# Expert products of a two-layer backbone: plain FP32 on 32-column tiles in place of three products of split halves on the full array

## Chip, cores and metric

The kernel runs on one core of a Trainium2 chip. The metric is the device time of one execution in microseconds (us); lower is better. Five engines matter here: PE (TensorE, matrix products), DVE (VectorE), ACT (ScalarE), POOL (GpSimd) and SP (SyncE, which here only issues transfers). Matrix products are written to PSUM (eight banks `ps[0]` to `ps[7]`, each 128 partitions by 512 FP32 columns); everything else lies in SBUF.

## What is computed

The reference runs 256 latent tokens and 256 context tokens, 1024 wide, through two layers of mixers (attention, pooling, Fourier) and a feed-forward part. In layer 0 the feed-forward part is dense; in layer 1 it is this mixture of experts over the 256 latent tokens, which the change touches:

```python
def swiglu(h, w1, w3, w2):
    return (jax.nn.silu(h @ w1) * (h @ w3)) @ w2

def moe_swiglu(h, w_router, b_router, w1, w3, w2):
    logits = (h @ w_router).astype(jnp.float32) + b_router.astype(jnp.float32)
    top_v, top_i = lax.top_k(logits, TOP_K)            # TOP_K = 2
    top_w = jax.nn.softmax(top_v, axis=-1)
    combine = jnp.sum(jax.nn.one_hot(top_i, N_EXPERTS) * top_w[..., None], axis=-2)
    out = jnp.zeros_like(h)
    for e in range(N_EXPERTS):                          # 8 experts, 1024 -> 2816 -> 1024
        out = out + combine[..., e:e + 1] * swiglu(h, w1[e], w3[e], w2[e])
    return out
```

All is FP32. With the reference's own inputs its router gives the eight experts 74, 80, 50, 73, 56, 53, 60 and 66 of the 256 tokens (each token goes to two).

## The kernel before

Everything up to the router is untouched by the change, but for the places of buffers. The expert stage comes last but for the final norm. It works on the tokens of one expert after the other: a table `sel` of ones and zeros picks them, products with it gather them into at most `SLOTS` = 128 rows, and, when an expert's rows are done, products with the turned table `selT` scatter them back (`gather`, `turned_select`, `scatter`). If any expert had more than `SLOTS` tokens, a second pass over all experts would run (`If(most_r[0] > SLOTS)`).

The weights of the experts come from memory in units of 1 MB (128 partitions by 2048 FP32), 33 units an expert, 264 in all, each read once. SP issues them in a fixed order into 11 landing buffers `estage` (L688); a buffer is free when DVE has read it (`e_lo_done`).

Precision is got by splitting: PE multiplies the type FP32R in one pass with fewer bits, so every FP32 operand is held as a high half (rounded to FP32R) and a low half (the rest), and three products stand for one: high x high, high x low, low x high. For the weights this is done anew for each unit: ACT writes the high half `ehi` (L992), then DVE writes the low half `elo` as the difference (L1548); both have three buffers (`SPLIT`). For the gathered tokens the halves are `xg_hi` and `xg_lo`, for the hidden rows `ehT_hi` and `ehT_lo`.

An expert is cut into 11 chunks of 256 hidden columns. A chunk has three units: "ga" and "gb" (the `w1` and `w3` columns of the chunk, four blocks of 128 rows each; `up`, L2204 to L2206: 12 products of 512 columns a unit) and "w" (256 rows of `w2`; `down`, L2218, L2219, L2224: 12 products of 512 columns). Between them ACT takes the silu (L1056), DVE multiplies by the other half of the bank (L1606), PE turns the 128 x 256 result with two transposes (`turn`, L2188), ACT and DVE split it (L1022, L1571). `down` of a chunk runs one chunk later than its `up`, so that PE need not wait for that.

At a few points of each expert PE does the other work: `gather` in two parts (8 products of 512 columns, L2160; 8 transposes, L2166), `turned_select` (L2179, L2181) and `scatter` (16 products of 256 columns, L2242, L2243), with the rows scaled and split by ACT (L1034) and DVE (L1580) beforehand.

After the last expert PE runs a few filling products (`keep_clock`, L1807), the last rows are scaled and split (L1091, L1648), scattered (L2306, L2307), added (L1657), squared (L734), summed (L1787) and normed.

One more place of the kernel is needed for the argument: `early_rows` (L1760 to L1770), near the start. It multiplies plain FP32 operands with only 32 columns on the weight side, and gives each of four such products its own quarter of the output partitions of one bank:

```python
for i in range(KD // quarters):                    # 2
    for q in range(quarters):                      # 4
        ins = pe.matmul(ps[2 + g][TILE_W * q:TILE_W * (q + 1), :], cond_32[:, k, :], w, ...)   # TILE_W = 32
```

Of the kernel before, what the change touches and what calls it, by code (L numbers as in the profile page):

```python
# [28 lines left out]
ACT = mybir.ActivationFunctionType  # L29
# [38 lines left out]
STAGE = 11  # L68
SPLIT = 3
# [37 lines left out]
assert UNITS % STAGE == 0 and UNITS % SPLIT == 0 and EXPERTS % PAIR == 0  # L107


SCATTER_AT = (1, 2)  # L110
GATHER_AT = (4, 6)
# [107 lines left out]
def direct_stream():  # L219
# [28 lines left out]
    "e_in": 16 * MOE_UNITS // STAGE, "e_hi_done": MOE_UNITS, "e_lo_done": MOE_UNITS, "e_used": MOE_UNITS,  # L248
    "et": _CHUNKS, "eu": _CHUNKS, "tr_full": _CHUNKS, "ehT_hi": _CHUNKS, "ehT_lo": _CHUNKS,
    "sel": 2 * EXPERTS, "ga_full": 2 * EXPERTS, "xrow": 2 * (EXPERTS - 1), "gt_full": 2 * EXPERTS, "xg_hi": 2 * EXPERTS, "xg_lo": 2 * EXPERTS,  # L250
    "st_full": EXPERTS, "selT": EXPERTS, "w_slot": EXPERTS,
    "y_hi_e": 2 * (EXPERTS - 1), "y_lo_e": 2 * (EXPERTS - 1), "sc_full": 4 * (EXPERTS - 1), "x_add": KD * (EXPERTS - 1),
}


def expert_steps(x):

    for c in range(CHUNKS):
        cc = x * CHUNKS + c
        for n, kind in enumerate(STEPS):  # L260
            if cc == 0 and kind == "w":
                continue
            yield (3 * cc - 1 + n if cc else n), cc, c, kind
# [41 lines left out]
def build(nc, A):  # L305
# [53 lines left out]
    warm = fixed.take("warm", [P, 2])  # L359
# [105 lines left out]
    ehi = ex.take("ehi", [P, SPLIT, 4 * 512], F32R)  # L465
    elo = ex.take("elo", [P, SPLIT, 4 * 512], F32R)

    et = ex.take("et", [P, 2, CW])
    eu = ex.take("eu", [P, 2, CW])
    ehT_hi = ex.take("ehT_hi", [P, 2, 2, SLOTS], F32R)  # L470
    ehT_lo = ex.take("ehT_lo", [P, 2, 2, SLOTS], F32R)
# [11 lines left out]
    posm = htok.take("posm", [P, 2, 2, 2 * EXPERTS])  # L483
# [4 lines left out]
    xg_hi = htok.take("xg_hi", [P, 2, KD, SLOTS], F32R)  # L488
    xg_lo = htok.take("xg_lo", [P, 2, KD, SLOTS], F32R)
# [84 lines left out]
    def pool_bank(g):  # L574

        return ps[(4, 5, 2, 3)[g]]

# [40 lines left out]
    def _(sp):  # L618
# [64 lines left out]
        def experts(p):  # L683

            def load(v0, w, at):

                sp.wait_ge(S("e_lo_done"), passed("e_lo_done", p) + v0 + (w + 1))
                sp.dma_start(estage[:, w % STAGE, :], at).then_inc(S(f"e_in{w % STAGE}"), 16)  # L688

            with sp.Fori(0, EXPERTS // PAIR) as e2:  # L690
                v0 = e2 * (PAIR * UNITS)
                for w in range(PAIR * UNITS):
                    load(v0, w, A["moe"][bass.ds(v0 + w, 1)].rearrange("a p n -> p (a n)"))
# [4 lines left out]
        with sp.If(most_r > SLOTS):  # L698
            experts(1)
# [7 lines left out]
    def _(act):  # L707
# [275 lines left out]

        act.sem_inc(S("e_used"), SPLIT)

        def experts(p):
            used = S("e_used")

            def hi(v0, w):
                act.wait_ge(S(f"e_in{w % STAGE}"), passed("e_in", p) + v0 * 16 + 16 * (w // STAGE + 1))  # L990
                act.wait_ge(used, passed("e_used", p) + v0 * STAGE + (w + 1))
                act.activation(ehi[:, w % SPLIT, :], estage[:, w % STAGE, :], ACT.Copy).then_inc(S("e_hi_done"), 1)  # L992

            def gathered_rows(e, x):

                for f in range(2):
                    act.wait_ge(S("ga_full"), passed("ga_full", p) + e * 2 + (2 * x + f + 1))
                    act.activation(xrow[:, f * 512:f * 512 + 512], ps[5 + f][:, :], ACT.Copy).then_inc(S("xrow"), 1)

            def first_hi(f):  # L1000

                act.wait_ge(S("ga_full"), passed("ga_full", p) + f + 1)
                act.activation(xg_hi[:, 0, 4 * f:4 * f + 4, :], ps[3 + f][:, :].rearrange("p (k s) -> p k s", s=SLOTS), ACT.Copy)\
                    .then_inc(S("xg_hi"), 1)

            def gathered_hi(e, x):

                for f in range(2):
                    act.wait_ge(S("gt_full"), passed("gt_full", p) + e * 2 + (2 * x + f + 1))
                    act.activation(xg_hi[:, x % 2, 4 * f:4 * f + 4, :], ps[5 + f][:, :].rearrange("p (k s) -> p k s", s=SLOTS), ACT.Copy)\  # L1010
                        .then_inc(S("xg_hi"), 1)

            def turned_select(e, x):

                act.wait_ge(S("st_full"), passed("st_full", p) + e + (x + 1))
                act.activation(selT[:, x % 2, :], ps[7][:, 0:SEQ], ACT.Copy).then_inc(S("selT"), 1)
                act.activation(w_slot[:, x % 2:x % 2 + 1], ps[7][:, SEQ:SEQ + 1], ACT.Copy).then_inc(S("w_slot"), 1)

            def hidden_hi(c_, pc):

                act.wait_ge(S("tr_full"), passed("tr_full", p) + c_ + (pc + 1))
                act.activation(ehT_hi[:, pc % 2, :, :], ps[2][:, pc % 2 * 256:pc % 2 * 256 + 256].rearrange("p (b s) -> p b s", s=SLOTS), ACT.Copy)\  # L1022
                    .then_inc(S("ehT_hi"), 1)

            def rows_hi(e, x, v0, w):

                act.wait_ge(used, passed("e_used", p) + v0 * STAGE + (SPLIT + w + 1))
# [1464 lines left out]
```

## Time and profile before

| | |
|---|---|
| time, median of 3 runs | 1940.72 us (1939.68 to 1941.45) |
| time of the profiled execution | 1937.46 us |
| its span | 1935.7 us |
| PE busy | 98% of the span |
| DVE busy | 71% |
| ACT busy | 51% |
| bytes moved by DMA | 438.21 MB |
| granted TensorE clock, mean | 0.997 |

The span runs from the first to the last instruction; the time has 1.76 us more around it. A row of the trace gives the start in us, the duration in us, the engine (PE for products, PEld for the weight loads that go ahead of each, SPq for SP's queue), the line of the kernel, what is written and read (buffer numbers left out) and how many rows were merged (x8). In brackets stands how long the engine was idle before it and what released it. One plain FP32 product of the program shows as two rows, each with its weight load; a product of FP32R operands shows as one. Ends of products are modelled, so the distance between starts tells more than their durations.

### The profile page before, as it was taken

The page shows a single profiled execution, that of the slowest core. Times are in us where ns is not written, and L with a number is a line of the kernel's source. Part 1 is how long each engine was busy: PE and PEld are TensorE (multiplying, and loading weights), DVE is VectorE, ACT ScalarE, POOL GpSimd, SP SyncE. Part 2 cuts the span into 40 slices and gives each one's busy share as a digit, 9 for nine tenths or more (in the row PEclk, how much of TensorE's full clock was granted, in tenths as well). Part 3 has the DMA queues.
Part 4 walks back from the last instruction along what each step waited for, and adds up shares of the span by engine and source line. Part 5 has one row for each costly group of instructions (what it writes and reads, how often), then busy time and mean ns, then how long its engine had stood idle before and what let it go on. Part 6 is the DMA issues. An engine that isn't in the chain of part 4 may idle for free.

```text
span 1935.7 us, 23955 instructions
## 1 busy us (share of the span) xinstructions
PE 1902.3 (98%) x9306; PEld 1525.0 (79%) x9306; DVE 1368.2 (71%) x1624; ACT 985.4 (51%) x1087; POOL 99.9 (5%) x127
## 2 busy tenths in 40 slices
PE   8999999999999999999999999999999999999997
PEld 6776666668788888878788988888888888888886
DVE  3783444477767555556454578989898989898996
ACT  4433323322432123243443377777777777777775
POOL 0160000000000001004000000000000000000000
PEclk9999999999999999999999999999999999999999
DMA  9412222354456557414334299989898999999990
GB/s 380 149 69 77 77 76 78 134 169 152 141 164 200 170 183 251 161 55 142 130 110 164 81 406 345 366 344 368 338 373 335 371 343 363 349 355 352 358 353 24
DMA packets 72834, 438.21 MB, mean 226 GB/s; under 512 B 9232, under 2 KB 10000, under 8 KB 28560
## 3 DMA queue, kind: packets, MB, share of 16 engines
q1 hardware_dynamic: 61056, 393.65, 54.1%
q0 software_dynamic: 11664, 43.00, 6.8%
q8 instruction: 76, 1.25, 0.3%
q14 instruction: 38, 0.31, 0.0%
HBM read 435.57 MB, written 1.05 MB: 226 GB/s over the span
## 4 chain that ended last, share of the span: by engine, by line
PE 91%; DVE 4%; ACT 3%; issue 1%; DMA 1%; SPq 0%; ACTq 0%; DVEq 0%
PE ps L1746 12%; PE ps L1747 12%; PE ps L1748 12%; PE ps L2204 8%; PE ps L2206 8%; PE ps L2205 8%; PE ps L2017 6%; PE ps L2218 4%; PE ps L2219 4%; PE ps L2224 4%; PE ps L1966 2%; PE ps L1923 2%; DVE wlo L1114 1%; PE ps L1992 1%; PE ps L1977 1%
## 5 line engine op out<-in xcount | busy, mean ns | idle before, releaser
L1548 DVE TENSOR_TENSOR elo<-estage,ehi 128x2048 fp32r<-128x2048 f32 x264 | 604.6, 2291 | 74.8 <-ACT ehi L992 74.0
L992 ACT ACTIVATE ehi<-estage 128x2048 fp32r<-128x2048 f32 x264 | 505.7, 1916 | 119.0 <-PE ps L2206 70.7
L1746 PE MATMUL ps<-h_hi,whi 128*128 128x512 f32 (+1 forms) x960 | 369.4, 385 | 10.2 <-DVE h_lo L1154 4.3
L1748 PE MATMUL ps<-h_hi,wlo 128*128 128x512 f32 (+1 forms) x960 | 344.9, 359 | 0.0
L1747 PE MATMUL ps<-h_lo,whi 128*128 128x512 f32 (+1 forms) x960 | 344.8, 359 | 0.0
L2204 PE MATMUL ps<-ehi,xg_hi 128*128 128x512 f32 x704 | 282.7, 402 | 1.0 <-DVE elo L1548 1.0
L2206 PE MATMUL ps<-ehi,xg_lo 128*128 128x512 f32 x704 | 275.4, 391 | 0.0
L2205 PE MATMUL ps<-elo,xg_hi 128*128 128x512 f32 x704 | 275.0, 391 | 0.0
L1114 DVE TENSOR_TENSOR wlo<-stage,whi 128x2048 fp32r<-128x2048 f32 x79 | 184.0, 2329 | 86.1 <-ACT whi L717 86.1
L717 ACT ACTIVATE whi<-stage 128x2048 fp32r<-128x2048 f32 x79 | 150.8, 1909 | 163.8 <-PE ps L1748 163.7
L1746 PEld LDWEIGHTS ps<-h_hi,whi 128*128 128x128 f32 x960 | 181.5, 189 | 54.1 <-issue 15.1
L1747 PEld LDWEIGHTS ps<-h_lo,whi 128*128 128x128 f32 x960 | 181.7, 189 | 35.8 <-issue 10.5
L1748 PEld LDWEIGHTS ps<-h_hi,wlo 128*128 128x128 f32 x960 | 181.5, 189 | 27.4
L2206 PEld LDWEIGHTS ps<-ehi,xg_lo 128*128 128x128 f32 x704 | 132.2, 188 | 28.1
L2204 PEld LDWEIGHTS ps<-ehi,xg_hi 128*128 128x128 f32 x704 | 132.3, 188 | 25.7 <-DVE elo L1548 1.4
L2205 PEld LDWEIGHTS ps<-elo,xg_hi 128*128 128x128 f32 x704 | 132.6, 188 | 24.3
L2218 PE MATMUL ps<-ehi,ehT_hi 128*128 128x512 f32 x352 | 137.9, 392 | 1.4 <-DVE elo L1548 0.9
L2219 PE MATMUL ps<-elo,ehT_hi 128*128 128x512 f32 x352 | 137.0, 389 | 0.0
L2017 PE MATMUL ps<-br,dw 128*128 128x512 f32 (+1 forms) x384 | 131.6, 485 | 0.0
L1241 DVE SCALAR_TENSOR_TENSOR gw<-gw,crow 128x1024 f32<-128x1024 f32 x80 | 98.8, 1244 | 25.3 <-DMA gw<-in_mods 25.3
L2224 PE MATMUL ps<-ehi,ehT_lo 128*128 128x512 f32 x352 | 108.4, 389 | 0.0
L2017 PEld LDWEIGHTS ps<-br,dw 128*128 128x128 f32 x384 | 71.0, 189 | 40.2 <-issue 34.5
(248 smaller groups left out, 2328.3 us busy)
## 6 DMA issues: line engine op xcount, KB each, us to landing
estage<-in_moe SPq DMA_DIRECT2D x264, 1024.0 KB, 5.1
stage<-in_split SPq DMA_DIRECT2D x79, 1024.0 KB, 5.2
gw<-in_mods POOLq DMA_DIRECT2D x80, 512.0 KB, 4.0
dw<-in_direct SPq DMA_DIRECT2D x36, 512.0 KB, 3.8
mw_a<-in_early SPq DMA_DIRECT2D x8, 512.0 KB, 7.9
mw_b<-in_early SPq DMA_DIRECT2D x8, 512.0 KB, 15.4
xT<-in_x SPq DMA_DIRECT2D x4, 512.0 KB, 5.4
gw<-in_cond_rows SPq DMA_DIRECT2D x1, 1024.0 KB, 17.7
```

The source lines that it names most:

```text
L992: act.activation(ehi[:, w % SPLIT, :], estage[:, w % STAGE, :], ACT.Copy).then_inc(S("e_hi_done"), 1)
L1114: dve.tensor_tensor(wlo[:, u % DENSE_SPLIT, :, :], stage[:, u % DENSE_STAGE, :].rearrange("p (b c) -> p b c", c=P), whi[:, u % DENSE_SPLIT ...
L1548: dve.tensor_tensor(elo[:, w % SPLIT, :], estage[:, w % STAGE, :], ehi[:, w % SPLIT, :], ALU.subtract)\
L1746: pe.matmul(out, hi, rhs_hi, start=first, stop=False)
L1747: pe.matmul(out, hi, rhs_lo, start=False, stop=False)
L1748: ins = pe.matmul(out, lo, rhs_hi, start=False, stop=last)
L2017: ins = pe.matmul(ps[1][:, 0:T - lc], dw[:, slot, 4 * (m % 2) + k, :], br[:, b, k, lc:T], start=(k == 0), stop=(k == KB - 1))
L2204: pe.matmul(o, xg_hi[:, x % 2, kk, :], hi[:, cols], start=(kk == 0), stop=False)
L2205: pe.matmul(o, xg_hi[:, x % 2, kk, :], lo[:, cols], start=False, stop=False)
L2206: ins = pe.matmul(o, xg_lo[:, x % 2, kk, :], hi[:, cols], start=False, stop=(kk == KD - 1))
L2218: pe.matmul(ps[3 + f][:, :], a_hi, hi[:, cols], start=first, stop=False)
L2219: pe.matmul(ps[3 + f][:, :], a_hi, lo[:, cols], start=False, stop=False)
```

## The change

The halves of the expert operands go: `up` and `down` multiply plain FP32 operands straight from the landing buffers, so `ehi`, `elo`, `xg_hi`/`xg_lo` and `ehT_hi`/`ehT_lo` and the work that made them are gone. `SLOTS` is 96, in three tiles of 32 tokens. A product takes 32 tokens on the weight side and has a quarter of the output partitions; four of them, with four different column blocks of the unit, fill the 128 partitions of a bank. An expert has three chunks (of 1024, 896 and 896 hidden columns): products of `up` have 512 columns in the first chunk and 448 in the others, those of `down` have 512. There are 35 units an expert and 280 in all, 16 of the 35 having 1792 columns instead of 2048, so the bytes stay the same. Each unit still has 12 products. The tokens' sums of `up` now stand with the hidden columns spread over the four quarters, so that DVE can turn them with one transpose of 32 x 32 blocks for each chunk (`gated`) and PE's `turn` is gone. The output rows of `down` come out in parts in two banks; `part_rows` on DVE puts them together (three copies, two additions) before they are scaled. A landing buffer is free when PE has read it (`e_used`); there are 14, of which the last three may be filled first when `htok_lo` is done. The gathered tokens are copied once instead of split. The final scatter uses four banks, and all sums of squares come behind it.

```diff
-STAGE = 11
-SPLIT = 3
+STAGE = 14
+LATE = 3
+TOK = 32
...
-CW = 256
-CHUNKS = FF // CW
-STEPS = ("ga", "gb", "w")
-UNITS = len(STEPS) * CHUNKS
-SLOTS = 128
+SLOTS = 96
+PASSES = -(-SEQ // SLOTS)
+TILES_E = SLOTS // TOK
+QUADS = P // TOK
+HWS = (256, 224, 224)
+CHUNKS = len(HWS)
+BLOCKS = [hw // TOK for hw in HWS]
+STARTS = [QUADS * sum(HWS[:c]) for c in range(CHUNKS)]
...
+DOWNS = [[(0, b) for b in range(8)], [(1, b) for b in range(6)], [(1, 6)] + [(2, b) for b in range(7)]]
+UNITS = CHUNKS * KD + sum(BLOCKS) // 2
...
-                sp.wait_ge(S("e_lo_done"), passed("e_lo_done", p) + v0 + (w + 1))
+                    sp.wait_ge(S("e_used"), passed("e_used", p) + v0 + (w + 1))
+                    if w == STAGE - LATE:
+                        sp.wait_ge(S("htok_lo"), 4)
...
-                act.activation(ehi[:, w % SPLIT, :], estage[:, w % STAGE, :], ACT.Copy).then_inc(S("e_hi_done"), 1)
...
+            def silu(c_, v0, x, c, upto):
+
+                cc = x * CHUNKS + c
+                act.wait_ge(used, passed("e_used", p) + v0 * STAGE + (STAGE + upto))
+                for t in range(TILES_E):
+                    act.activation(et[:, cc % 2, t * HWS[c]:(t + 1) * HWS[c]], up_bank(x, c, t)[:, 0:HWS[c]], ACT.Silu).then_inc(S("et"), 1)
...
-                dve.tensor_tensor(elo[:, w % SPLIT, :], estage[:, w % STAGE, :], ehi[:, w % SPLIT, :], ALU.subtract)\
...
+        def part_rows(done, count):
+
+            for n, (b, q) in enumerate(((3, 3), (4, 0), (4, 3))):
+                dve.tensor_copy(y_d[n * TOK:(n + 1) * TOK, :], ps[b][q * TOK:(q + 1) * TOK, :]).then_inc(done, 1)
+            for n in (1, 2):
+                rows = slice(n * TOK, (n + 1) * TOK)
+                dve.wait_ge(done, count + n + 1)
+                dve.tensor_tensor(y_d[rows, :], y_d[rows, :], ps[4][rows, :], ALU.add).then_inc(done, 1)
+            dve.wait_ge(done, count + 5)
...
+            def gated(c_, x, c):
+
+                cc, n = x * CHUNKS + c, HWS[c]
+                for t in range(TILES_E):
+                    dve.wait_ge(S("et"), passed("et", p) + c_ * TILES_E + (TILES_E * cc + t + 1))
+                    cols = slice(t * n, (t + 1) * n)
+                    dve.tensor_tensor(eu[:, cc % 2, cols], et[:, cc % 2, cols], up_bank(x, c, t)[:, n:2 * n], ALU.mult).then_inc(S("eu"), 1)
+                dve.wait_ge(S("eu"), passed("eu", p) + c_ * TILES_E + TILES_E * (cc + 1))
+                dve.transpose(ehT[:, c, 0:TILES_E * n], eu[:, cc % 2, 0:TILES_E * n]).then_inc(S("ehT"), 1)
...
-                    pe.matmul(o, xg_hi[:, x % 2, kk, :], hi[:, cols], start=(kk == 0), stop=False)
-                    pe.matmul(o, xg_hi[:, x % 2, kk, :], lo[:, cols], start=False, stop=False)
-                    ins = pe.matmul(o, xg_lo[:, x % 2, kk, :], hi[:, cols], start=False, stop=(kk == KD - 1))
+            def landed(v0, w):
+
+                pe.wait_ge(S(f"e_in{w % STAGE}"), passed("e_in", p) + v0 * 16 + 16 * (w // STAGE + 1))
+                return estage[:, w % STAGE, :]
+
+            def up(v0, w, x, c, kk):
+
+                rows, n = landed(v0, w), 2 * HWS[c]
+                for t in range(TILES_E):
+                    for q in range(QUADS):
+                        ins = pe.matmul(up_bank(x, c, t)[q * TOK:(q + 1) * TOK, 0:n], xg[:, x % 2, kk, t * TOK:(t + 1) * TOK],
+                                        rows[:, q * n:(q + 1) * n], start=(kk == 0), stop=(kk == KD - 1))
...
+            def down(v0, w, d):
+
+                for u in range(len(DOWNS[d]) // 2):
+                    rows = landed(v0, w + u)
+                    two = DOWNS[d][2 * u:2 * u + 2]
+                    first, last = (d, u) == (0, 0), d == CHUNKS - 1 and u == len(DOWNS[d]) // 2 - 1
+                    for i, (c, b) in enumerate(two):
+                        for q in range(QUADS):
+                            t, f = (q, 0) if q < TILES_E else (0, 1)
+                            pe.matmul(ps[3][q * TOK:(q + 1) * TOK, :], turned(c, b, t), rows[:, i * D + f * 512:i * D + f * 512 + 512],
+                                      start=(first and i == 0), stop=(last and i == 1))
+                    for q in range(QUADS):
+                        t, i = 1 + q // 2, q % 2
+                        ins = pe.matmul(ps[4][q * TOK:(q + 1) * TOK, :], turned(*two[i], t), rows[:, i * D + 512:i * D + D], start=first, stop=last)
+                    ins.then_inc(used, 1)
```

## Rows read from the trace of the kernel before

**Rows 1.** The page: busy tenths of PE and DMA in 40 slices.

```profile
PE   8999999999999999999999999999999999999997
...
DMA  9412222354456557414334299989898999999990
```

**Rows 2.** Stretches: from:to, length, engines' busy us (instructions), clock, DMA share, GB/s.

```profile
1133.30:1917.30 784.00, 780.94 (x3618) 643.94 (x3616) 702.25 (x549) 582.14 (x504) 0.00 (x0) 1.00 0.89 342
...
1450.00:1550.00 100.00, 100.00 (x467) 82.71 (x466) 90.50 (x71) 74.41 (x65) 0.00 (x0) 1.00 0.92 354
```

**Rows 3.** The page's costliest groups: busy us, mean ns, idle before, releaser.

```profile
L1548 DVE TENSOR_TENSOR elo<-estage,ehi 128x2048 fp32r<-128x2048 f32 x264 | 604.6, 2291 | 74.8 <-ACT ehi L992 74.0
...
L2204 PE MATMUL ps<-ehi,xg_hi 128*128 128x512 f32 x704 | 282.7, 402 | 1.0 <-DVE elo L1548 1.0
```

**Rows 4.** Order of time: two neighbouring expert products of 512 columns.

```profile
1502.44 0.39 PE L2204 MATMUL ps<-ehi,xg_hi 128*128 128x512 f32 x1
...
1502.67 0.39 PE L2205 MATMUL ps<-elo,xg_hi 128*128 128x512 f32 x1
```

**Rows 5.** Order of time, near the start: packed FP32 products of L1769.

```profile
15.21 0.16 PEld L1769 LDWEIGHTS ps<-mw_a,cond 128*32 128x32 f32 x8 [2.22 <-DMA mw_a<-in_early]
...
15.67 0.13 PEld L1769 LDWEIGHTS ps<-mw_a,cond 128*32 128x32 f32 x4 [0.30 <-issue]
16.10 0.13 PEld L1769 LDWEIGHTS ps<-mw_a,cond 128*32 128x32 f32 x4 [0.30 <-issue]
17.07 0.52 PEld L1787 LDWEIGHTS ps<-ones,sq_ends 128*128 128x128 f32 x4 [0.84 <-issue]
...
35.78 0.40 PE L1748 MATMUL ps<-h_hi,wlo 128*128 128x512 f32 x1
...
36.11 1.92 PE L1769 MATMUL ps<-mw_b,cond 128*32 128x512 f32 x16
...
37.97 0.50 PE L1746 MATMUL ps<-h_hi,whi 128*128 128x512 f32 x1
```

**Rows 6.** Stretches, columns as in the second group: DMA engines full.

```profile
15.00:24.00 9.00, 8.62 (x66) 4.79 (x67) 1.31 (x7) 1.01 (x3) 0.00 (x0) 1.00 1.03 418
...
1115.00:1150.00 35.00, 34.06 (x231) 30.27 (x230) 26.16 (x47) 26.95 (x35) 0.00 (x0) 1.00 1.01 425
```

**Rows 7.** Order of time, layer 1: 256-column products, then 64 weight columns.

```profile
1014.84 0.28 PE L1746 MATMUL ps<-h_hi,whi 128*128 128x256 f32 x1
...
1014.96 0.28 PE L1747 MATMUL ps<-h_lo,whi 128*128 128x256 f32 x1
...
1017.74 0.42 PEld L1992 LDWEIGHTS ps<-pT,v_a 128*64 128x64 f32 x8 [0.33 <-issue]
...
1018.12 0.47 PEld L1992 LDWEIGHTS ps<-pT,v_b 128*64 128x64 f32 x8
...
1018.76 0.42 PEld L1977 LDWEIGHTS ps<-ident,prob 128*128 128x128 f32 x4 [0.17 <-issue]
```

**Rows 8.** Order of time: first expert weights issued, first expert product.

```profile
1109.64 64.80 SPq L688 DMA_DIRECT2D estage<-in_moe  x25
...
1133.34 0.19 PEld L2204 LDWEIGHTS ps<-ehi,xg_hi 128*128 128x128 f32 x1
```

**Rows 9.** Order of time: an expert's eight transposes.

```profile
1195.49 1.03 PE L2166 MATMUL ps<-ident,xrow 128*128 128x128 f32 x8
```

**Rows 10.** Groups by line, expert stage: what follows an `up` product.

```profile
L1606 DVE TENSOR_TENSOR eu<-et,ps 128x256 f32<-128x256 f32 x88 | 36.4, 413 | 0.9 <-ACT et L1056 0.9
...
L1056 ACT ACTIVATE et<-ps 128x256 f32<-128x256 f32 x88 | 33.8, 384 | 63.6 <-PE ps L2206 63.6
```

**Rows 11.** Order of time, after the last expert product.

```profile
1917.29 1.27 ACT L1091 ACTIVATE y_rows<-ps,w_slot 128x512 fp32r<-128x512 f32 x2 [3.15 <-PE ps L2224]
1918.01 1.41 DVE L1648 SCALAR_TENSOR_TENSOR y_rows<-ps,w_slot,y_rows 128x512 fp32r<-128x512 f32 x2 [3.41 <-ACT y_rows L1091]
...
1920.02 0.36 PE L2306 MATMUL ps<-selT,y_rows 128*128 128x256 f32 x1
```

More of the change, by code:

```diff
@@ L698, in _ @@
         with sp.If(most_r > SLOTS):
-            experts(1)
+            for p in range(1, PASSES):
+                experts(p)
         for name, count, k in (("out_d", 2, 2), ("out_a", 2, 0), ("out_d", 4, 6), ("out_a", 4, 4)):
@@ L1096, in _ @@
         with act.If(most_r[0] > SLOTS):
-            last_rows_hi("fx")
-            experts(1)
-        last_rows_hi("fn")
+            for p in range(1, PASSES):
+                last_rows_hi(p, "fx", p - 1)
+                experts(p)
+        last_rows_hi(1, "fn", 0)
         for k in range(KD):
@@ L1526, in most_of_all @@
         def most_of_all():
-            step(dve.tensor_scalar(posm[:, 1, :, 0:EXPERTS], place, float(SLOTS), None, ALU.subtract))
+            for n in range(1, PASSES):
+                step(dve.tensor_scalar(posm[:, n, :, 0:EXPERTS], place, float(n * SLOTS), None, ALU.subtract))
             dve.wait_ge(S("most_full"), 1)
@@ L1663, in _ @@
         with dve.If(most_r[0] > SLOTS):
[L1664 to L1668 removed]
+            for p in range(1, PASSES):
+                last_rows_lo(p, "fx", p - 1)
+                last_adds("fx", p - 1)
+                experts(p)
+        last_rows_lo(1, "fn", 0)
+        last_adds("fn", 0)
         norm("fin", SEQ)
@@ new lines, in first_gather, with gather_rows @@
+                    ins.then_inc(S("gt_full"), 1)
+            def gather_rows(e, x):
+                pe.wait_ge(S("sel"), passed("sel", p) + e * 2 + 2 * (x + 1))
+                if x >= 2:
+                    pe.wait_ge(S("x_add"), passed("x_add", p) + e * KD + (KD * (x - 2) + 6))
+                else:
+                    pe.wait_ge(S("eu"), passed("eu", p) + TILES_E)
+                for f in range(2):
+                    for t in range(2):
+                        for n, rows in enumerate((htok_hi, htok_lo)):
+                            ins = pe.matmul(ps[6 + f][0:SLOTS, :], sel[:, t, :], rows[:, t, f * 512:f * 512 + 512],
+                                            start=(t == 0 and n == 0), stop=(t == 1 and n == 1))
+                    ins.then_inc(S("ga_full"), 1)
@@ L2266, in expert @@
+                            pe.wait_ge(S("xg"), passed("xg", p) + e * 2 + 2 * (x + 1))
+                        if (x, c) not in ((0, 0), (0, 1)):
+                            pe.wait_ge(S("eu"), passed("eu", p) + c_ * TILES_E + TILES_E * (x * CHUNKS + c))
+                        for kk in range(KD):
+                            if c == 1 and kk == KD // 2 and x >= 1:
+                                scatter(e, x, (0, 1, 2))
+                            up(v0, w + kk, x, c, kk)
                         if c == 1:
@@ L2322, in _ @@
         with pe.If(most_r[0] > SLOTS):
-            last_scatter("fx")
-            experts(1)
+            for p in range(1, PASSES):
+                last_scatter("fx", p - 1)
+                experts(p)
         keep_clock(2, 6)
-        last_scatter("fn")
-        for k in range(KD // 2, KD):
+        last_scatter("fn", 0)
+        for k in range(KD):
             last_squares(k)
```

458 lines of the change are left out of this document (191 added, 267 removed).

## The prediction, made before the change was run

> **What bounds the kernel now.** I read the page's slices first: PE is busy in all of them, and DMA is at 9 tenths only in the last two fifths, the expert stage [rows 1]. Then the stretches [rows 2]: from the first expert product to the last, 784 us, PE is busy for 781, DVE for 702, ACT for 582, at full granted clock, and the DMA engines move 354 GB/s in mid-stage at a share of 0.92. Three resources are near their ends, so the question is which wait ends last. The groups answer [rows 3]: PE waits 1.0 us in all for DVE's low halves ahead of L2204, while DVE waits 74 us for ACT, and ACT in turn for PE. So PE sets the pace, DVE (2.29 us a unit) has some slack, and the loads follow as buffers come free. The 90% of DVE that the change frees is not the bound and by itself is worth nothing. What PE does is: 264 units x 12 products = 3168 products, one every 0.23 us. Their starts are 0.23 apart to two digits [rows 4]; over a run of ten the trace gives 0.2275. That is 720.7 us of the 784. The rest: 176 turns at 0.11 (eight transposes in 1.03 us less the tail of the last, about 0.87 [rows 9]) are 19.4; per expert change, of which there are seven, the gather's 8 products (1.82), 8 transposes (0.87), the turned selection (0.7) and 16 scatter products of 256 columns at 0.12 [rows 7] (1.92) are 5.3, so 37; the last 7 us are small waits and the first expert's selection.
>
> **What the new products cost.** The packed form is in the trace of before already: `early_rows` multiplies plain FP32 with 32 weight columns, four products to a bank, 512 columns each [rows 5]. Eight products (16 rows of the trace) begin at 15.21; their weight loads come as eight, then four at 15.67 and four at 16.10. A round of four tiles thus takes 0.43 us for one of the two halves of a product (0.46 for the first one, which starts the run), 0.86 for four whole products. So four tiles truly run side by side. DMA was full at that time, 418 GB/s [rows 6], which is the company that the expert products will have. A unit has 12 products, three rounds: 2.58 us at 512 columns; 2.26 at 448 (scaled by columns; an estimate). Per expert 8 + 11 units of 2.58 and 16 of 2.26 are 85.1 us, for eight experts 681. Against 720.7 + 19.4 for products and turns now, that is 59 less. This is smaller than it looks: 96 slots in place of 128 and four passes in place of three cancel, and the gain is the 14 ns by which an FP32R product exceeds its share of the columns, and the turns.
>
> **What is added on PE.** Packed and full products alternate. From the packed ones to a full one: 36.11 to 37.97 is 1.86 for eight products that should take 1.72, so 0.14; into them: 35.78 to 36.11 is 0.33 where 0.23 was due, so 0.10 [rows 5]. Each expert change has three excursions (scatter, the last scatter with the gather, the turned rows): 7 x 3 x 0.24 = 5. Gather, turned rows, selection and scatter keep their counts: 37. For small waits I keep 4 of the 7. Stage: 681 + 37 + 5 + 4 = 727, which is 57 less than 784. Its start stays at 1133.3 [rows 8]: the first gather, not the halves of the weights, is the long part before it.
>
> **What lies beside.** ACT: three silus a chunk at about 0.38, DVE three multiplications at 0.41 [rows 10], and a turning of 768 columns, for which no row exists: between 0.86 us (elementwise by the 2.29 us for 2048 columns [rows 3]) and three times that. Together 3 to 5 us, covered by the `down` that stands between two `up`s, 3 or 4 units or 7.7 to 10.3 us. The next `up` waits only for the multiplications. If that cover failed, each of 24 chunks would cost what is over it. The joined output rows (`part_rows`, five steps of 512 columns, each at most 0.75 as a DVE step of 128 x 512 [rows 11]), then scaling and splitting, take some 5.5 us; four units of `up` (9 us) cover them before the scatter, and DVE has nothing else queued there but the next selection. The three additional landing buffers, and SP's wait for `htok_lo` with all later loads behind it, cost nothing as long as the first 11 units feed PE: they are issued from 1109.64, and PE starts 24 us later [rows 8].
>
> **The loads.** 276.8 MB remain. PE at full pace takes 1.05 MB in 2.58 us or 0.92 in 2.26, 406 GB/s, and 381 over the stage. With buffers asked for as fast as they come, the engines moved 425 GB/s for 35 us, with all of ACT's and DVE's splitting beside them [rows 6]. So they can follow, with a margin of 5% at the peak and 11% in the mean, and 14 buffers to smooth it.
>
> **After the last product.** Before: last product's end 1917.3, second low half 1919.4 [rows 11]. After: five steps of DVE (3.5 us), two scalings of 0.75 with ACT's second between: 5.0. So 3 us more. Scatter into four banks, then all squares at the end: what one saves the other costs, I take zero. A clock falling in that gap would be one more us or two, so 3 to 5.
>
> **The sum.** 57 - 3 = 54 less. The profiled execution has 1937.46; 1883.5. The median shown is 3.3 above it: 1887.
>
> **Rivals.**
>
> *Partial gain, because the loads or the rounds are slower.* The DMA rate in mid-stage is 354 at a share of 0.92 [rows 2], 385 at a full share, not 425. At 385 the mean demand of 381 is barely met, and little changes; at 360 the 276.8 MB from 1109.6 take 769 us, end at 1878.6, and PE ends some 3 us later, 21 us later than forecast: 1908. For it: a share of 0.92 looks nearly full. Against: the 425 of rows 6. Or each half round takes the 0.46 of the first instead of 0.43: 681 becomes 729, time 1935, no change. Against: the second and third are at 0.43, and the end at 17.07 fits 0.43.
>
> *Slower, because the sequencer of PE can't feed it.* A unit now has 12 weight loads and 12 products; then 24 and 24, in 2.58 us, one each 54 ns; in the 448-column units one each 47 ns. The quickest long run of the trace is a pair each 0.12 us, 60 ns a row [rows 7], and though weight loading explains that too, no long run shows less. At 60 ns a unit takes 2.88 us, 280 of them 806; with 46 us of the rest 852, which is 68 more than now, with 3 behind it 71: 2012. It decides above 55 ns a row (280 x 48 x 0.055 + 46 = 785). Against it: 16 loads and 16 products with 64 weight columns go by from 1017.74 to 1018.76, 32 ns each [rows 7]. That is a short burst, which a queue could have held ready, as it could the 32 of `early_rows`.
>
> The Trainium skill (TensorE: Matmul & The Clock Gate, on the back-to-back floor) gives a sequencer cost of about 62 ns per matmul where decoding is not done in hardware. If it counts for products alone, an estimate by it is 24 x 62 ns = 1.5 us a unit, and nothing changes; if for weight loads too, it is 3.0 us a unit and the kernel is slower by this rival's mechanism.
>
> *Slower, because four tiles aren't four times as fast in a long run.* Were a round 1.08 us instead of 0.86, the products would take 681 x 1.26 = 855 us, the stage 901, the time 2061. It decides above 0.93 us a round (46 us over 681 is 7%, and turns the gain to nothing with the tail's 3). Against: rows 5, where two rounds fit 0.86 each; but two rounds are all that there is.
>
> The same page (Measured speedup vs the span model) speaks against the change: three 32-column tiles gave 2.38 times, not 3. Read as a steady rate, 79% of the ideal, it is this rival, at 1.08 us a round. The trace doesn't bear it out at its two rounds.
>
> *The change doesn't do what it says.* Above 96 tokens in one expert a second pass would read all weights again, some 700 us. The router's largest count for the reference's inputs is 80, so I give it no chance.
>
> **How the numbers follow.** Forecast, 1868 to 1900: 64%. Partial gain, 1900 to 1935: 16%, of which a fifth lies within 0.2% of 1940.7. Sequencer, about 2010: 12%. Tiles, about 2060: 5%. Better than 1868 (no cost of the excursions, no waits): 3%. The range has to keep 8 in 10: 1866 to 1928 holds the forecast and most of the partial gain; the two slower rivals are left out. About 0.2% is what a measurement here can tell from no change. Faster 0.80, same 0.03, slower 0.17.
>
> **What would show it.** Weight loads of the new `up` in fours 0.43 us apart (0.38 in the second and third chunk), and a stretch of the stage with PE's weight loading far less busy. The stage 727 us long. ACT and DVE below a third. DMA at 380 GB/s in mid-stage. PE's waits: hardly any for `eu`, `ehT` or `estage`. If PE's idle time ahead of `up` names DMA, the loads are the bound; if it names nothing ("issue") and the fours stand further apart than 0.43, it is the sequencer or the tiles: at 448 columns the sequencer would make them as far apart as at 512, slow tiles would not. Wrong I would be, above all, if two rounds of packed products don't tell what a thousand do.

## The result and the profile after

The changed kernel takes 1887.3 us (median of 4 runs, 1882.9 to 1889.9) against 1940.5 before (the runs of "Time and profile before" and one more): a ratio of 0.9726, with a 95% interval from 0.9714 to 0.9738. The profiled execution has 1886.42 us, its span 1884.6.

The page of the changed kernel, cut to its line of busy times and the lines that answer to [rows 1] and [rows 3]:

```profile
PE 1852.9 (98%) x12682; PEld 1135.7 (60%) x12682; DVE 773.4 (41%) x1305; ACT 452.7 (24%) x719; POOL 99.9 (5%) x127
...
PE   8999999999999999999999999999999999999997
PEld 5776666667788888887788994333333333333334
DVE  3683444478667645545655451020202020202022
...
DMA  9422212255255546532333449999999999999980
...
L2204 PE MATMUL ps<-estage,xg 128*32 128x448 f32 (+1 forms) x4608 | 459.1, 557 | 0.0
...
L2204 PEld LDWEIGHTS ps<-estage,xg 128*32 128x32 f32 x4608 | 148.9, 110 | 302.4 <-issue 301.3
L1599 DVE TENSOR_TENSOR eu<-et,ps 128x224 f32<-128x224 f32 (+1 forms) x72 | 24.4, 394 | 502.8 <-ACT et L1050 502.8
```

PE is as busy as before, and its idle time ahead of the packed products (L2204) is nothing. DVE falls from 71 to 41% of the span and is nearly idle in the expert stage; PE's weight loading falls from 8 tenths to 3. Two stretches of the stage, with the columns of [rows 2]: DMA now moves 377 to 384 GB/s in mid-stage where it moved 354.

```profile
1450.00:1550.00 100.00, 100.00 (x958) 35.27 (x958) 16.89 (x35) 8.37 (x22) 0.00 (x0) 1.00 0.97 377
1550.00:1650.00 100.00, 100.00 (x978) 34.46 (x970) 14.27 (x29) 6.33 (x17) 0.00 (x0) 1.00 0.98 384
```

The rhythm itself: weight loads of the upward products in order of time, four at a time, as in [rows 5].

```profile
1400.04 0.13 PEld L2204 LDWEIGHTS ps<-estage,xg 128*32 128x32 f32 x4 [0.30 <-issue]
1400.46 0.13 PEld L2204 LDWEIGHTS ps<-estage,xg 128*32 128x32 f32 x4 [0.30 <-issue]
1400.89 0.13 PEld L2204 LDWEIGHTS ps<-estage,xg 128*32 128x32 f32 x4 [0.30 <-issue]
```

Loads of four, 0.43 us apart, after hundreds of such rounds: what two rounds of `early_rows` showed holds in a long run. And one expert change with its three stops, in order of time (PE only):

```profile
1430.08 9.20 PE L2204 MATMUL ps<-estage,xg 128*32 128x448 f32 x96
1439.21 0.38 PE L2242 MATMUL ps<-selT,y_rows 96*128 96x256 f32 x1
...
1440.83 9.23 PE L2204 MATMUL ps<-estage,xg 128*32 128x448 f32 x96
1449.98 0.39 PE L2242 MATMUL ps<-selT,y_rows 96*128 96x256 f32 x1
...
1452.53 1.92 PE L2222 MATMUL ps<-estage,ehT 128*32 128x512 f32 x16
...
1462.85 18.22 PE L2204 MATMUL ps<-estage,xg 128*32 128x448 f32 x192
1481.01 0.88 PE L2179 MATMUL ps<-ident,xrow 96*128 96x96 f32 x8
...
1482.29 1.92 PE L2222 MATMUL ps<-estage,ehT 128*32 128x512 f32 x16
...
1490.04 20.78 PE L2204 MATMUL ps<-estage,xg 128*32 128x512 f32 x192
1510.64 1.90 PE L2222 MATMUL ps<-estage,ehT 128*32 128x512 f32 x16
```

Eight units of 448 columns take 18.16 us (1462.85 to 1481.01), 2.27 each with the way out of them; eight of 512, which run on into packed products of `down`, take 20.60 (1490.04 to 1510.64), 2.575 each. The three stops (PE leaving the packed products for work on the full array) cost what lies between the end of one packed run and the start of the next: 1.67 us (a run of four units from 1430.08 would end at 1439.16; the next starts at 1440.83), 2.62 and 1.28, together 5.57.

The first expert product and what follows the last one, to set beside [rows 8] and [rows 11]:

```profile
1137.89 18.66 PE L2204 MATMUL ps<-estage,xg 128*32 128x512 f32 x172
...
1859.65 1.04 PE L2226 MATMUL ps<-estage,ehT 128*32 128x512 f32 x8
1860.76 0.68 ACT L1094 ACTIVATE y_rows<-ps,w_slot 96x512 fp32r<-96x512 f32 x1 [15.65 <-PE ps L2226]
1860.76 2.13 DVE L1554 COPY y_d<-ps 32x512 f32<-32x512 f32 x3 [15.74 <-PE ps L2226]
1861.54 1.60 PE L1814 MATMUL ps<-ident,ones 128*128 128x128 f32 x12 [0.85 <-issue]
1862.92 1.40 DVE L1558 TENSOR_TENSOR y_d<-y_d,ps 32x512 f32<-32x512 f32 x2
...
1865.91 0.47 PE L2304 MATMUL ps<-selT,y_rows 96*128 96x256 f32 x1 [2.76 <-DVE y_rows L1654]
1866.18 0.42 PE L2305 MATMUL ps<-selT,y_rows 96*128 96x256 f32 x1
...
1869.38 6.82 PE L1794 MATMUL ps<-ones,sq_fin 128*128 128x1 f32 x32
```

The stage runs from 1137.9 to 1860.5 (1859.65 and two half rounds of 0.43; a half round is one row from each of the four tiles, since a product shows as two rows), 722.6 us, and the tail to the end of the span takes 24.1. Before it was 784.0 and 18.4, counted to the first reading of the last sums (1917.3); counted to the end of the last product, as here, 783.8 and 18.6.

### The profile page after: what moved, and what is told of

It reads as the page before. It is cut to its first block, busy times and chain, and to the rows that moved or that the text cites. A ratio compares the mean times of both kernels' runs of the same rounds, so it can differ in the third digit from the quotient of the medians.

```text
span 1884.6 us, 29697 instructions
## 1 busy us (share of the span) xinstructions
PE 1852.9 (98%) x12682; PEld 1135.7 (60%) x12682; DVE 773.4 (41%) x1305; ACT 452.7 (24%) x719; POOL 99.9 (5%) x127
## 4 chain that ended last, share of the span: by engine, by line
PE 92%; DVE 4%; ACT 2%; issue 1%; DMA 1%; SPq 0%; ACTq 0%; DVEq 0%
PE ps L2204 24%; PE ps L1753 12%; PE ps L1755 12%; PE ps L1754 12%; PE ps L2222 8%; PE ps L2024 7%; PE ps L2226 4%; PE ps L1973 2%; PE ps L1930 2%; DVE wlo L1120 1%; PE ps L1999 1%; PE ps L1984 1%; ACT whi L743 1%; PE ps L1952 1%; PE ps L1938 1%
## 5 line engine op out<-in xcount | busy, mean ns | idle before, releaser
L2204 PE MATMUL ps<-estage,xg 128*32 128x448 f32 (+1 forms) x4608 | 459.1, 557 | 0.0
L2204 PEld LDWEIGHTS ps<-estage,xg 128*32 128x32 f32 x4608 | 148.9, 110 | 302.4 <-issue 301.3
L1599 DVE TENSOR_TENSOR eu<-et,ps 128x224 f32<-128x224 f32 (+1 forms) x72 | 24.4, 394 | 502.8 <-ACT et L1050 502.8
L2222 PE MATMUL ps<-estage,ehT 128*32 128x512 f32 x1408 | 167.5, 593 | 0.0
L1050 ACT ACTIVATE et<-ps 128x224 f32<-128x224 f32 (+1 forms) x72 | 21.2, 367 | 561.1 <-PE ps L2204 561.1
L2222 PEld LDWEIGHTS ps<-estage,ehT 128*32 128x32 f32 x1408 | 44.2, 110 | 99.2 <-issue 98.6
L2226 PE MATMUL ps<-estage,ehT 128*32 128x512 f32 x704 | 91.6, 592 | 0.0
L1753 PE MATMUL ps<-u_hi,whi 128*128 128x512 f32 x176 | 68.5, 389 | 0.0
L1754 PE MATMUL ps<-u_lo,whi 128*128 128x512 f32 x176 | 68.5, 389 | 0.0
L1755 PE MATMUL ps<-u_hi,wlo 128*128 128x512 f32 x176 | 68.5, 389 | 0.0
L1688 POOL DMA_DIRECT2D gw<-in_mods x80 | 42.4, 530 | 421.6 <-DVE gw L1247 407.7
```

Of the source, the lines that this page charges most:

```text
L1688: pool.dma_start(gw[:, u % 2, :], A["mods"][u]).then_inc(S(f"mod_in{u % 2}"), 16)
L1753: pe.matmul(out, hi, rhs_hi, start=first, stop=False)
L1754: pe.matmul(out, hi, rhs_lo, start=False, stop=False)
L1755: ins = pe.matmul(out, lo, rhs_hi, start=False, stop=last)
L2204: ins = pe.matmul(up_bank(x, c, t)[q * TOK:(q + 1) * TOK, 0:n], xg[:, x % 2, kk, t * TOK:(t + 1) * TOK], rows[:, q * n:(q + 1) * n], start ...
L2222: pe.matmul(ps[3][q * TOK:(q + 1) * TOK, :], turned(c, b, t), rows[:, i * D + f * 512:i * D + f * 512 + 512], start=(first and i == 0), st ...
```

## Experiments

The theory: PE sets the pace on both sides; the packed plain FP32 products run at the rate of their columns, and the gain is that rate against 0.2275 us for each FP32R product, and the turns. Its rivals: the loads, the sequencer of PE, tiles that don't truly overlap, and, for the size of the gain, DVE's work. Kernels whose name begins with a_ change the changed kernel, those with b_ the one before. The two-tile kernel, the one with the other order and the three with cut columns were run once each; the executions of one kernel spread over up to 10 us here (1881.6 to 1891.1 for the changed one), so of those five only differences well above that count.

**Do the tiles overlap: two tiles instead of four.**

```diff
-ins = pe.matmul(up_bank(x, c, t)[q * TOK:(q + 1) * TOK, 0:n], ...
+ins = pe.matmul(up_bank(x, c, t)[q % 2 * TOK:(q % 2 + 1) * TOK, 0:n], ...
```

> The changed kernel with the upward products on two column tiles instead of four (the second two column blocks are added onto the first two, so the hidden part is another; as many products, columns and bytes as before). If four tiles really run side by side, two take twice as long: half a round's four products 0.86 us instead of 0.43, the stage 454 us longer, 2341. If the gain came from something else than the tiles, the time changes by less than that; if from nothing in them, 1887.

2338.0 us, against 2341 expected. Weight loads of this kernel in order of time:

```profile
1399.96 0.12 PEld L2204 LDWEIGHTS ps<-estage,xg 128*32 128x32 f32 x2 [0.26 <-issue]
1400.34 0.12 PEld L2204 LDWEIGHTS ps<-estage,xg 128*32 128x32 f32 x2 [0.26 <-issue]
1400.71 0.12 PEld L2204 LDWEIGHTS ps<-estage,xg 128*32 128x32 f32 x2 [0.26 <-issue]
```

Two loads each 0.375 us (448 columns) where four tiles have four in 0.38. So the speed of the upward products goes with the number of tiles at work: with two of them the kernel is 20% slower than the one before.

**Does it depend on the order of the products.**

```diff
-                for t in range(TILES_E):
-                    for q in range(QUADS):
+                for q in range(QUADS):
+                    for t in range(TILES_E):
```

> The changed kernel with the two loops of the upward products swapped: for one column tile after the other its three products come together, instead of one product for each of the four tiles by turns. Same products, same sums. If each tile has a queue of its own, or PE looks far enough ahead, tiles still overlap: 1887. If products start in the order of the program and a tile takes one at a time, six halves of 0.43 us follow each other on a tile before the next tile gets work, and neighbours overlap only by one: some 9 us a unit instead of 2.58, and a time of 2800 to 3100. In between lies a limited look ahead.

2091.0 us, 204 more than the changed kernel, between the two expectations. Neither of the two limiting cases holds. Weight loads in order of time, then PE with a run of four units:

```profile
1400.05 0.17 PEld L2204 LDWEIGHTS ps<-estage,xg 128*32 128x32 f32 x4 [0.24 <-issue]
1400.46 0.14 PEld L2204 LDWEIGHTS ps<-estage,xg 128*32 128x32 f32 x2 [0.24 <-issue]
1400.83 0.17 PEld L2204 LDWEIGHTS ps<-estage,xg 128*32 128x32 f32 x4 [0.24 <-issue]
...
1410.34 14.17 PE L2204 MATMUL ps<-estage,xg 128*32 128x448 f32 x96
1424.44 0.39 PE L2242 MATMUL ps<-selT,y_rows 96*128 96x256 f32 x1
```

Six loads each 0.78 us, where eight would go by: about three tiles at work instead of four, so 3.12 us a unit. On all upward products (455 us in the changed kernel) that is a third more, 152 us. The rest lies at the ends of each run of products, where fewer tiles have work: four units take 14.10 us and not 12.5, 1.6 more, and with four such runs an expert that is some 51. Together 203. So products of other tiles do start while one tile has more of its own to do, but not without limit; how PE does that, no run here shows. Taking turns among the tiles, as the change does, is a part of what makes it pay; it is worth 204 us here.

**Is PE's sequencer near: fewer columns for each product.** Half of them here; in the second kernel a quarter (`// 4` in both places).

```diff
-                rows, n = landed(v0, w), 2 * HWS[c]
+                rows, n = landed(v0, w), 2 * HWS[c] // 2
-            return QUADS * 2 * HWS[c]
+            return QUADS * 2 * HWS[c] // 2
```

> As the kernel with half the columns, and only half the columns of those units loaded (185 MB in the stage), so that PE is the bound again; the rest of the hidden part is left out. If the columns alone set a round, half a round of 256 columns takes 0.216 us, the stage 505 us, time 1669. If the sequencer of PE needs some 50 to 60 ns for each weight load and product, a unit stays at 2.4 to 2.9 us and the time between 1890 and 1990.

1662.2 us; the stage 503 (1134.1 to 1636.8), as the columns alone say, 0.216 us for a half round of 256.

> A quarter of the columns (128 and 112) in the products of the upward half, and a quarter loaded; the rest of the hidden part is left out. Columns alone: 0.109 us for half a round, stage 390 us, time 1556. The four weight loads of half a round, 0.13 us in the trace, may now be the longer part: 0.13, 36 us more, 1592. A sequencer limit of 30 ns a row would give 0.24 for half a round and 1740.

1596.4 us, at the second of the three expected times, but not for its reason. One run of 128-column products of this kernel, and a stop with what follows it:

```profile
1395.80 5.42 PE L2204 MATMUL ps<-estage,xg 128*32 128x128 f32 x192
1401.04 1.90 PE L2222 MATMUL ps<-estage,ehT 128*32 128x512 f32 x16
...
1416.74 0.58 PE L2242 MATMUL ps<-selT,y_rows 96*128 96x256 f32 x1 [2.92 <-DVE y_rows L1581]
1417.12 0.42 PE L2243 MATMUL ps<-selT,y_rows 96*128 96x256 f32 x1
...
1419.60 4.25 PE L2204 MATMUL ps<-estage,xg 128*32 128x112 f32 x96
```

192 rows of products (96 products, two rows each) and as many weight loads in 5.24 us: 0.109 us for four of each, again just the columns, 14 ns a row. The sequencer rival needed 55 and falls by a factor of four. The 40 us above the columns' 1556 come from elsewhere. 22 us are PE's wait for the joined output rows in seven stops, since the cover of four units, 9 us in the changed kernel, is now 2.5. And after each of these waits PE runs for a while at half clock (0.50 from 1417 to 1419): six times the scatter takes 2.86 us instead of 1.62, and the four units behind it take 3.1 to 4.2 us, in all seven some 11 us more than at full clock. Together that is 19 us, and 41 with the wait. The cover that the prediction named for `part_rows` is therefore real, and what is over it is paid twice, once as a wait and once in the clock.

**Where is the limit of the loads.** Columns cut to half as above, all loads kept.

```diff
-                rows, n = landed(v0, w), 2 * HWS[c]
+                rows, n = landed(v0, w), 2 * HWS[c] // 2
```

> The changed kernel with the products of the upward half cut to half their columns (256 and 224), all loads as they are; the other columns of the hidden part are left out. PE's stage falls to some 505 us, so the loads set the pace and show their limit. At the 425 GB/s of the first fill 276.8 MB take 651 us from 1114: span 1792, time 1794. At 385, if a share of 1 in mid-stage is no more than that: 719 us, time 1862.

1805.8 us. Stretches:

```profile
1250.00:1350.00 100.00, 80.50 (x1098) 36.26 (x1094) 14.28 (x29) 6.33 (x17) 0.00 (x0) 1.00 1.01 425
1450.00:1550.00 100.00, 79.52 (x1046) 35.09 (x1038) 16.34 (x33) 7.26 (x20) 0.00 (x0) 1.00 1.01 425
```

PE now waits 259 us for `estage`, and the engines move 425 GB/s for 600 us, the rate of [rows 6]. The 12 us above 1794 are in part my omission: the last seven units are `down`, uncut, and take PE 18.0 us without a wait (1763.0 to 1781.0), so PE ends 12 us after the loads would at 425 GB/s, and not 3. The rest is a first fill that began at 1118 and not at 1114. So with these buffers and this order the loads allow 1806, 81 us below the changed kernel, and its 380 GB/s at a share of 0.98 is PE's pace and not their limit.

**Fewer landing buffers.**

> The changed kernel with 10 landing buffers instead of 14. Theory: PE sets the pace and ten units ahead are 25 us of cover, so no change, 1887 within 3. Rival: the loads run close to their limit (mid-stage share 0.98) and the depth of the buffers is what keeps PE fed: 10 us slower or more, with PE idle ahead of its first product of a unit and DMA named.

```diff
-STAGE = 14
+STAGE = 10
```

1888.2 us (ratio to before 0.9736, 0.9716 to 0.9756; the changed kernel beside it 0.9729, 0.9707 to 0.9751). No difference that can be told: the buffers beyond ten bring nothing, and the partial-gain rival by way of the loads falls.

**What was DVE's work worth.**

```diff
-dve.tensor_tensor(elo[:, w % SPLIT, :], estage[:, w % STAGE, :], ehi[:, w % SPLIT, :], ALU.subtract)
+dve.tensor_tensor(elo[:, w % SPLIT, 0:512], estage[:, w % STAGE, 0:512], ehi[:, w % SPLIT, 0:512], ALU.subtract)
-... lo[:, cols] ...
+... lo[:, 0:512] ...
```

> The kernel before, with the low halves of the weights made for a quarter of the columns only (DVE 512 instead of 2048 a unit) and that quarter used four times over by PE: DVE loses some 440 us of work, PE keeps each of its products. Theory: PE's products set the pace and 0.2275 us each is their own cost: 1940 within 3. Rival: the 14 ns a product above the 213 that the columns take come from DVE's traffic to the same memory, or DVE paces PE: each product at 0.216, 36 us less, 1904.

1935.6 us, ratio 0.998 (0.997 to 0.9989): 3 to 4 us less, at the edge of what was expected. The products still start 0.2275 us apart:

```profile
1499.82 0.40 PE L2205 MATMUL ps<-elo,xg_hi 128*128 128x512 f32 x1
...
1501.87 0.39 PE L2205 MATMUL ps<-elo,xg_hi 128*128 128x512 f32 x1
```

(nine products in 2.05 us), with DVE busy 38% of the time in mid-stage and no longer 91%. So the 14 ns above the columns are not this work of DVE, and what goes is small waits: the stage of this run is 780.0 us (1134.7 to 1914.7) where [rows 2] has 784, and of PE's three waits for DVE, 2.5 us in the trace of before, none is left. That this part of DVE's splitting was worth 3 to 4 us is shown; that the rest of it and ACT's half are worth as little was not tried.

**What do 96 slots do without tiles.**

```diff
-                    o = ps[cc % 2][:, :]
+                    o = ps[cc % 2][0:96, :]
-                    ... xg_hi[:, x % 2, kk, :] ... xg_lo[:, x % 2, kk, :] ...
+                    ... xg_hi[:, x % 2, kk, 0:96] ... xg_lo[:, x % 2, kk, 0:96] ...
```

> The kernel before, with 96 weight columns and 96 output partitions instead of 128 in its upward products (2112 products; slots above 96 are left as they are, and no expert has more than 80 tokens). If a product on the full array takes the time of its 512 moving columns whatever the number of weight columns, 96 slots alone bring nothing: 1939 within 3. The changed kernel's own gather products with 96 weight columns start 0.235 us apart instead of 0.2275; if that is their cost, 16 us more, 1955. If fewer weight columns cut the time (a weight load of 96 takes less), the 14 ns above the columns shrink, up to 30 us less, 1910.

1943.4 us, ratio 1.0016 (1.0005 to 1.0028), nearest to the first expectation. Order of time:

```profile
1501.13 0.39 PE L2204 MATMUL ps<-ehi,xg_hi 128*96 128x512 f32 x1
...
1502.28 0.39 PE L2206 MATMUL ps<-ehi,xg_lo 128*96 128x512 f32 x1
```

Five products in 1.15 us, 0.230 each: 2 ns more, not less, on 2112 products, and 3.3 us more in the time than the kernel before beside it (1940.1). Fewer slots on the full array bring nothing. Of the two forms run here, three quarters of the slots are three quarters of the work only in tiles.

**The tail.**

```diff
-        keep_clock(2, 6)
+        keep_clock(2, 18)
         last_scatter("fn", 0)
```

> The changed kernel as it is, for comparison with the others of this group: 1887 us. Last expert product to the end of the span 24 us, with the granted clock at 0.5 from the last scatter on.

> The changed kernel with 18 filling products instead of 6 behind the last expert product. Theory: the tail is longer than forecast because PE idles 2.8 us while DVE joins the output rows, and the granted clock falls to 0.5; kept up, the 16 scatter products take 1.9 us and not 3.4, the sums of squares 3.8 and not 6.8, the last pair 0.5 less: 5 us less, 1882. Rival: the tail is set by DVE's additions and ACT's squares, and the clock costs nothing: 1887, or 1 us more for the filling.

1882.7 against 1887.7 us in the same group, five runs each, but their ranges overlap (1880.0 to 1889.0, 1881.6 to 1891.1). So the times alone don't show a gain. The two profiled executions: stretches of the changed kernel's tail first, then this kernel's.

```profile
1868.00:1872.00 4.00, 4.00 (x21) 4.00 (x21) 2.50 (x6) 2.82 (x7) 0.00 (x0) 0.50 0.00 0
1872.00:1876.00 4.00, 4.00 (x20) 4.00 (x20) 0.00 (x0) 0.00 (x0) 0.00 (x0) 0.50 0.00 0
```

```profile
1868.00:1872.00 4.00, 2.84 (x26) 2.76 (x25) 3.02 (x5) 0.72 (x1) 0.00 (x0) 1.00 0.01 4
1872.00:1876.00 4.00, 4.00 (x38) 4.00 (x36) 2.76 (x8) 2.24 (x6) 0.00 (x0) 1.00 0.00 0
1876.00:1880.00 4.00, 2.79 (x20) 2.71 (x20) 1.28 (x6) 1.12 (x4) 0.00 (x0) 0.66 0.00 0
```

With the filling the clock is at its full 2.4 GHz when the scatter and the first sums run (0.12 us from start to start instead of 0.21), and the tail is 21.4 us instead of 24.1. It is not all to be had: the filling holds up the scatter until 1.3 us after DVE is done, and the stretch from 1876 has a clock of 0.66, before the sums are over.

**All four parts of the scatter in one stop (banks 5, 6, 7 and 4), with the filling.**

```diff
-                                scatter(e, x, (0, 1, 2))
+                                scatter(e, x, (0, 1, 2, 3))
...
-                            if x >= 1:
-                                scatter(e, x, (3,))
...
-        keep_clock(2, 6)
+        keep_clock(2, 18)
```

> The changed kernel as it is, measured beside the next one on the same chip: 1887 us.

> The changed kernel with 18 filling products behind the last expert product, and with all four parts of an expert's scatter in one place (the fourth in bank 4, free by then). A way out of the packed products costs 0.15 us and a way in 0.09 in the changed kernel's trace. The second stop remains for the gather, so of the stops two remain and only their content moves. Theory: this part gives between 0 and 1.7 us; with the 5 of the filling, 1880 to 1883. Rival: the fourth part's additions, which now stand ahead of DVE's multiplications, hold back the next upward products: slower than 1883.

1880.5 against 1887.3 us, and here no run of one (1878.7 to 1884.2) lies among those of the other (1885.0 to 1888.6); ratio to the kernel before 0.9692 (0.9672 to 0.9712). It is the fastest of all that was run. Its parts aren't settled: from the first upward product to the last the profiled executions have 703.8 and 704.2 us, so fusing gives 0.4, DVE's additions hold nothing back, and the tail is 21.4, of which 2.0 are filling that goes on after DVE is done. The execution beside it had a tail of only 19.5, because there the granted clock held until the sums were nearly done (1.00 to 1872, 0.92 from there to 1876) with 6 filling products alone:

```profile
1869.12 0.39 PE L2304 MATMUL ps<-selT,y_rows 96*128 96x256 f32 x1 [2.49 <-DVE y_rows L1654]
...
1871.13 3.63 PE L1794 MATMUL ps<-ones,sq_fin 128*128 128x1 f32 x32
```

These two executions are 4.2 us apart. The tail is 1.9 us longer with the filling, and what outweighs it lies ahead of the expert stage, in code that is the same: the stage begins at 1135.4 with it and at 1141.1 without, where the granted clock from 15 to 25 us is 1.00 and 0.50. Over all five runs of each the mean granted clock is 0.994 to 0.998 with this kernel and 0.991 to 0.993 with the other. Where the 6.8 us between the medians arise, and whether the filling brings them, stays open.

## Why the prediction was right, step by step

The forecast was 1887 for the median, the result 1887.3. That this agrees to the last digit is luck: the forecast of the profiled execution is 2.9 us too low, and its distance to the median was taken 2.4 too large. The terms:

| us | forecast | measured |
|---|---|---|
| packed products of the stage | 681 | 682 (8 x (19 x 2.575 + 16 x 2.27)) |
| stops at seven expert changes | 37 + 5 | 39 (7 x 5.57) |
| small waits and the first selection | 4 | 1.6 (the rest of 722.6) |
| stage | 727 | 722.6 |
| start of the stage | 1133.3 | 1137.9 |
| tail behind the last product | 21.4 | 24.1 |
| span | 1881.7 | 1884.6 |
| profiled execution | 1883.5 | 1886.4 |
| median above it | 3.3 | 0.9 |

*What bounds the kernel* held. PE waits for nothing in the stage but 0.5 us once, and taking three quarters of DVE's largest job away moved the old kernel by 3 to 4 us only.

*The cost of the new products* was the term on which all rested, read from sixteen rows of the trace near its start, and it is right to 1 us in 681. The sequencer and the tiles, the two rivals for slower, needed these two rounds not to tell what a thousand do. (The tile rival's threshold of 0.93 us a round is right, but the slack is 54 us over 681, 8%, and not the 46 and 7% written there.) The shorter products (14 ns a row) and the two-tile kernel show that they do. The figure of the Trainium skill (TensorE: Matmul & The Clock Gate, Measured speedup vs the span model), 2.38 times for three tiles, isn't borne out as a steady rate: a half round of four tiles takes 0.43 us, within 1% of the columns of one product (2 x 512 at 2.4 GHz, 0.427). What the prediction did not see is that this hangs on the order of the products: with the tiles' products bunched, 204 us more.

*The stops* were priced at 0.24 us each time beside their content, and all of 6.0 us a change was 5.57. *Small waits* of 4 us were too many: 3 to 4 us of the 7 in the old kernel went with DVE's low halves in the experiment, 2.5 of them as waits of PE for DVE that the trace names.

*The covers* held: no wait for `eu`, `ehT`, `xg` or the joined rows shows for PE (its weight loading waited for `ehT` once, 0.4 us). DVE's turning of 768 columns, put between 0.86 and 2.6 us for want of a row, takes 0.98.

*The loads* held in size: 380 GB/s in mid-stage. The margin was put at 5 to 11% from [rows 6], and the loads-bound kernel confirmed the 425 over 600 us. The partial-gain rival leant on the share of 0.92 in [rows 2] as if it were nearly full. It is now 0.98 at 380 GB/s and 1.01 at 425: it does not tell how far off the limit is.

*The tail* is the step whose size was off. Its 21.4 us are the 18.4 of before and 3 for joining the output rows; the scatter with the squares behind it, and the clock, were set at nothing, the clock with "one more us or two" in the range. The last product of the kernel before, to count both from the same event:

```profile
1916.64 0.61 PE L2224 MATMUL ps<-ehi,ehT_lo 128*128 128x512 f32 x2
```

It ends at 1917.1 (two products of 0.23), 2.9 us ahead of the scatter [rows 11]. After the change this takes 5.4 us: 2.5 more, near the 3 forecast. From the scatter to the end were 15.7 us before; in the execution in which the clock held they are 14.1, so the scatter into four banks and the squares behind it save 1.6 us where zero was taken. In the changed kernel's profile they are 18.7: PE idles 2.8 us ahead of the scatter, and the 16 scatter products, the 32 rows of sums (6.8 us in place of 3.6) and what follows run at half clock. So the clock costs 4.6 us here, neither nothing nor two, and 2.5 - 1.6 + 4.6 is the 5.5 by which the tail grew. Four profiled executions have this tail with 6 filling products and all loads and columns: three have 24.1 or 24.2 us and one 19.5, after idle times of 2.3 to 2.8 us in all of them. What decides between them isn't shown.

*The start* is 4.6 us later, which no step foresaw. From the norm's last product ahead of the router to the first expert product it is 20.7 us before and 20.9 after (one more small DVE step for the third pass's slots, which the prediction did not list). The other 4.3 arise in code that is the same: the packed products at 16 us took 3.56 us instead of 1.92, and the stretches 480 to 500 and 840 to 860 have a granted clock of 0.91. The profiled executions of the eleven kernels with the change begin the stage at 1134.1 to 1143.0, those of the three without it at 1133.2 to 1134.7. Much of this is the clock of the single execution, then; whether the change also makes the low clock early on more frequent (it shows between 15 and 25 us in seven of the eleven, and in none of the three, of which one has 0.84 from 25 to 35) isn't settled. Start and tail took 4.6 and 2.7 us more than forecast, against 4.4 less in the stage: that is the 2.9 us of the span.

Of the chances, the 3% for no change was taken out of "1900 to 1935", a range that ends below the 1936.8 from which on a time would count as no change.

## What to carry to other kernels

If a precise product is made of three passes over the full array and its weight side has no more than 96 columns in use, price the plain form on 32-column tiles: three tiles of slots for four passes, the same column time, and all the splitting and its buffers gone. Let the products take turns among the tiles, keep what is not packed in few blocks, and look at every gap of PE that the new form opens, the tail's above all. When a change frees an engine that is not the bound, expect its small waits back and little more: here 3 to 4 us for three quarters of DVE's largest job.

## What the runs showed of the hardware

- Four column tiles of 32 run side by side at twice the rate of two: four half products take the columns of one, over hundreds of rounds, at 512, 448, 256 and 128 columns (0.43, 0.38, 0.216 and 0.109 us for a half round), if neighbouring products go to different tiles; with three in a row for each tile it is about three at a time (six loads in 0.78 us at 448 columns).
- Weight loads and products of this kind were issued at 14 ns a row for 384 rows (5.24 us), far below the 60 ns that the trace of before could vouch for.
- A plain FP32 half product takes 0.4292 us for 512 columns (20.60 us for 48), 0.6% above the 0.4267 that its columns take twice over at 2.4 GHz; an FP32R product 0.2275, 6.6% above the 0.2133 of its columns once, with DVE busy 91% or 38% beside it, and with 96 weight columns 0.230.
- Into packed products PE loses about 0.1 us (1440.62 to 1440.83 for a product of 0.12) and out of them about 0.2, each time: 45 half rounds of 448 columns take 16.91 us by the distance of their weight loads, so 48 take 18.04 and not 18.16, and the first full product takes 0.22 us to the next where the others take 0.12.
- The DMA engines gave 425 GB/s for 600 us with loads of 7 and 8 KB a partition; their busy share was 0.98 already at 380.
- PE ran at half clock after it had idled 2.9 us in the stops of the kernel with a quarter of the columns, and after 2.3 to 2.8 us in three executions of the tail; after 2.5 us in a fourth it ran at full clock.
